# Cached attention of the sample streams with its operands swapped: queries stationary in four column groups

## The chip, the cores and the metric

The kernel runs on one core of a Trainium2 chip. The metric is the device time of one execution in microseconds. The kernel before was run three times: 2839.32, 2842.61 and 2842.74 us, median 2842.61 us.

## What is computed

One layer of a streaming encoder on two groups of tokens: a prompt of 256 tokens, and a sample group of 8 running streams with 16 new tokens each (128 rows together). All data is float32. The part that the change touches is the attention of the sample group over its cached keys and values:

```python
# sample group: 8 streams, 16 queries each, 128 cached keys and values per stream and head
kk = concatenate([cache_k, k])            # (8 streams, 128 + 16 keys, 8 heads, 128)
s  = einsum("bqhd,bkhd->bhqk", q, kk) / sqrt(128) + bias   # A: learned bias of the distance
s  = s + c_q - c_k                                         # B: sums of log forget gates
p  = softmax(s)                                            # over cached and own keys
y  = einsum("bhqk,bkhd->bqhd", p, concatenate([cache_v, v]))
```

There are 8 heads of kind A (bias by distance) and 8 of kind B (forget gates). After it come the gated branch projections, the output projection and, for every token, a mixture of experts: queries, keys, the best 16 of 256 candidates per retrieval head, and 128 gathered rows of two tables for each token.

## The kernel before

One core does everything, with an order written out by hand for each of the five engines and for the DMA queues, tied together by semaphores. `front(S)` (sample, 128 rows) comes first on TensorE, then `front(R)` (prompt, 256 rows); behind them stand the experts of the prompt. The sample's experts are worked on by VectorE between the steps of `front(R)`.

A front has four groups G of four heads each (G 0 and 1 are kind A, 2 and 3 kind B). A group needs three chunks of the input projection (queries, keys, values), each 2048 x 512 weights in four pieces of 1 MB that the sync queue loads into a ring of four (`wring`). A piece is four float32 matmuls with 512 moving columns (`part`, L600). The pieces of the next group's query and key chunks are laid between the attention steps of the present group by `fill()`, eight in all, so that TensorE has work while VectorE and ScalarE do the softmax.

For each head of the sample the steps are:

- `cached_scores(j)` (L661): for each of the 8 streams one matmul, with the stream's cached keys stationary (128 columns) and its 16 queries moving. The result lies with the keys on the partitions, in bank 3 of PSUM. For kind B, L659 first adds the sums of the cached forget gates.
- ScalarE copies that to `cst` (L994), and `scores(j)` turns it with an identity matmul into block 0 of bank 4 or 5 (L686), where L672 has put the scores of the new keys in block 1 and L683 the forget gates (kind B).
- `bias(j)` on VectorE adds biases and masks (L1327, or L1334 and L1335 for kind B) and takes the maximum of a row (L1343), ScalarE takes the exponent (L1000), `norm(j)` divides (L1352, L1355).
- `turn_probs(j)` (L698) transposes the two blocks of probabilities, ScalarE copies them (L1006), and `values(j)` (L716, L718) has the new values and then, for each stream, its cached values stationary with 16 probability columns moving. The result is already turned: ScalarE copies it to `yT` (L1012).

Two heads are in flight: the scores of head j+2 are made after the values of head j. Behind the last head of the front TensorE waits for `y_copied` and for the sigmoids of ScalarE (L1038) before it goes on to the branch projections.

GpSimd makes the masks at the start (`CONSTS` counts them) and loads the cached keys and values of the next group when `st_done` and `y_done` say that the present ones are used up (`load_caches`).

Of the kernel before, what the change touches and what calls it, by code (L numbers as in the profile page):

```python
# [52 lines left out]
CONSTS = 16  # L53
# [40 lines left out]
class Front:  # L94
# [3 lines left out]
    def __init__(self, sem, name, tiles, chunk0, streams):  # L98
        self.tiles, self.n, self.tokens, self.chunk0, self.streams = tiles, len(tiles), len(tiles) * P, chunk0, streams
        self.v_bank = 1 if streams else 0  # L100
        self.blocks = 2 if streams else 3

        self.segments = [(0, 2)] if streams else [(0, 1), (1, 2)]
# [16 lines left out]
        self.st_done = sem(f"st_done_{name}")  # L120
        self.st_copied = sem(f"st_copied_{name}")
# [7 lines left out]
        self.y_done = sem(f"y_done_{name}")  # L129
        self.y_copied = sem(f"y_copied_{name}")  # L130
# [68 lines left out]
def build(nc, a):  # L199

    with ExitStack() as ctx:
# [30 lines left out]
        cst = fold[:, 11 * P:13 * P].rearrange("p (w n) -> p w n", w=2)  # L232
# [13 lines left out]
        hnw = sb("hnw", [P, 2, HC])  # L246
        ranks = sb("ranks", [P, 2 * TOPK + 1], U32)
# [174 lines left out]
        def _(pool):  # L422
# [50 lines left out]
            def load_caches(G):  # L473
# [3 lines left out]
                for sm, dst, src, used in ((cache_loaded[0], ckT, a[k], S.st_done), (cache_loaded[1], cv, a[w], S.y_done)):  # L477
# [112 lines left out]
        def _(pe):  # L590
# [29 lines left out]
            def group(F, G, fill):  # L620
# [44 lines left out]
                def scores(j):  # L665
# [5 lines left out]
                    if F.streams:  # L671
                        mm(A[:, P:2 * P], q_of(j, 0), F.kT[:, j, :], start=True, stop=True, **sk)  # L672
                        f = F.lfb[:, 0, j, :] if br else None
                        extra = ((1, f, ntriB), (1, triB, f), (0, triB, f)) if br else ()
                    else:
                        mm(A[:, 0:P], q_of(j, 0), F.kT[:, j, 0:P], start=True, stop=True, **sk)
                        mm(A[:, P:3 * P], q_of(j, 1), F.kT[:, j, :], start=False, stop=True, **sk)
# [3 lines left out]
                    last = None  # L681
                    for m, left, right in extra:
                        last = mm(A[:, m * P:(m + 1) * P], left[:, :], right[:, :], start=False, stop=True, **sk)  # L683
                    if F.streams:
                        pe.wait_ge(F.st_copied, H + 1)
                        last = mm(A[:, 0:P], cst[:, j % 2, :], ident[:, :], start=False, stop=True, **sk)  # L686
                    elif last is None:

                        last = mm(A[:, 3 * P:3 * P + 1], ident[:, :], ident[:, 0:1], start=False, stop=True, **sk)
# [12 lines left out]
                def values(j):  # L702
                    H = H0 + j
                    pe.wait_ge(F.pt_copied, H + 1)
                    if H:
                        pe.wait_ge(F.y_copied, H)
# [19 lines left out]
                def score(j):  # L726
                    if F.streams:
                        cached_scores(j)
                    scores(j)

                score(0)
                if G == 1:
                    pe.wait_ge(F.z_ready, 1)
                score(1)
                fill()
                for j in range(HC):
                    turn_probs(j)
                    if j + 2 < HC:
                        if F.streams:
# [18 lines left out]
            def front(F):  # L758
# [13 lines left out]

                pe.wait_ge(F.y_copied, 2 * HEADS)
# [129 lines left out]
        def _(act):  # L903
# [35 lines left out]
            def front(F, experts):  # L939
# [14 lines left out]

                for G in range(2 * GROUPS):
                    H0, br, cols = HC * G, "ab"[G // GROUPS], slice((G % GROUPS) * CW, (G % GROUPS + 1) * CW)
                    for c in range(2):
# [7 lines left out]
                        if c:  # L965
                            place(2 * n * G, F.qT, F.turned, F.placed)
# [24 lines left out]
                    def copy_cached(j):  # L991
                        if F.streams:
                            act.wait_ge(F.st_done, H0 + j + 1)
                            act.activation(cst[:, j % 2, :], ps[:, 3, 0:P], ACT.Copy).then_inc(F.st_copied, 1)  # L994

# [755 lines left out]
```

## Time and profile before

| | |
|---|---|
| median of three runs | 2842.61 us (2839.32 to 2842.74) |
| span of the profiled execution | 2835.0 us |
| that execution's own time | not given apart from the three runs, which lie 4.3 to 7.7 us above the span |
| instructions | 19569 |
| TensorE busy | 2098.1 us (74%) |
| VectorE busy | 1870.1 us (66%) |
| GpSimd busy | 1254.9 us (44%) |
| ScalarE busy | 500.9 us (18%) |
| attention of the sample, by the rows of L661 and L718 | 66.7 to 314.2 us after the start |

PE is TensorE, PEld its weight loads, DVE is VectorE, ACT is ScalarE, POOL is GpSimd. A row of the timeline gives start and length in us, then engine, line, operation, output and inputs, and how many instructions were merged. A float32 matmul leaves two records of each kind, a transpose one. The ends of matmuls are modelled, so the step from one start to the next is the time that an instruction really takes from its followers. [...]

### The profile page before, as it was taken

Reading aid. Unit: us, or ns where it says so; the run is one execution under the profiler, and the core shown is the slowest. Engines: PE = TensorE matmul, PEld = TensorE weight load, DVE = VectorE, ACT = ScalarE, POOL = GpSimd, SP = SyncE. Lnnn points to the kernel's source line nnn. Section 1 sums busy time; section 2 is a strip of 40 time slices with the busy share of each in tenths; the row PEclk is TensorE's granted clock in tenths of the full one; section 3 lists DMA queues with packets and bytes.
Section 4 is the critical chain, followed back from the end, with each engine's and each line's share of the span. In section 5 each row is a group of like instructions: output and inputs, shape, how many; then the busy total and the mean of one; then the engine's idle time right before and its main releaser. Section 6 shows DMA issues by size and latency. Waiting matters only on the chain.

```text
span 2835.0 us, 19569 instructions
## 1 busy us (share of the span) xinstructions
PE 2098.1 (74%) x6070; PEld 1056.1 (37%) x6070; DVE 1870.1 (66%) x2615; ACT 500.9 (18%) x1187; POOL 1254.9 (44%) x855
## 2 busy tenths in 40 slices
PE   7999999999999898988899920000341038999996
PEld 3665544444545443333344410000331025444443
DVE  1222000396777757657666899999999998666666
ACT  1212100112222210000001100000995243000000
POOL 2000000023444445435444367776777866454444
PEclk9999999999999999989999965555555568999998
DMA  9777688989999999999999999999999998999999
GB/s 362 282 289 260 211 292 300 309 331 366 367 396 398 402 377 382 409 395 393 411 384 374 409 389 407 407 408 385 383 405 411 422 367 303 409 405 410 409 404 353
DMA packets 271465, 1047.11 MB, mean 369 GB/s; under 512 B 19856, under 2 KB 19856, under 8 KB 203280
## 3 DMA queue, kind: packets, MB, share of 16 engines
q0 software_dynamic: 113792, 697.85, 61.1%
q1 hardware_dynamic: 154880, 343.97, 33.3%
q10 hardware_dynamic: 2704, 4.21, 0.4%
q8 instruction: 44, 0.72, 0.1%
q14 instruction: 45, 0.37, 0.0%
HBM read 1036.50 MB, written 9.45 MB: 369 GB/s over the span
## 4 chain that ended last, share of the span: by engine, by line
PE 39%; DVE 25%; DMA 24%; POOL 5%; issue 5%; ACT 1%; POOLq 0%; SPq 0%; DVEq 0%; ACTq 0%
PE ps L600 34%; DMA yTr<-in_peer_v,fold 12%; DVE bigs L1612 7%; DVE bigr L1612 6%; DMA bigr<-in_w_br_a 4%; DVE hr L1643 3%; POOL bigr L571 3%; DMA bigr<-in_w_out 2%; DMA bigs<-in_peer_v,idxnow 2%; DVE spare L1612 2%; DMA bigr<-in_w_in 2%; DVE pwork L1425 1%; PE ps L661 1%; PE ps L718 1%; DVE bigs L1549 1%
## 5 line engine op out<-in xcount | busy, mean ns | idle before, releaser
L600 PE MATMUL ps<-bigr 128*128 128x512 f32 x1920 | 862.1, 607 | 43.5 <-DMA bigr<-in_w_in 21.7
L600 PEld LDWEIGHTS ps<-bigr 128*128 128x128 f32 x1920 | 368.3, 195 | 497.4 <-issue 442.7
L524 POOL DMA_INDIRECT bigs<-in_peer_u,idxnow x128 | 230.7, 1802 | 551.1 <-DVE bigs L1559 531.8
L600 PE MATMUL ps<-bigr,bigs 128*128 128x512 f32 x896 | 406.1, 608 | 20.3 <-DMA bigr<-in_w_in 16.7
L1643 DVE SCALAR_TENSOR_TENSOR hr<-yTr,fold,hr 128x1024 f32<-128x1024 f32 x205 | 263.5, 1286 | 136.8 <-DMA yTr<-in_peer_v,fold 134.4
L1549 DVE SCALAR_TENSOR_TENSOR bigs<-bigs,acts 128x2048 f32<-128x2048 f32 x128 | 300.9, 2350 | 67.4 <-DMA bigs<-in_peer_v,idxnow 67.1
L1559 DVE SCALAR_TENSOR_TENSOR bigs<-bigs 128x2048 f32<-128x2048 f32 x128 | 293.0, 2290 | 63.8 <-DMA bigs<-in_peer_u,idxnow 62.4
L581 POOL DMA_INDIRECT yTr<-in_peer_v,fold x205 | 219.6, 1071 | 207.0 <-DVE hr L1643 197.6
L1612 DVE SCALAR_TENSOR_TENSOR bigr<-bigr 128x2048 f32<-128x2048 f32 x122 | 275.8, 2288 | 5.9 <-DMA bigr<-in_peer_u,fold 5.2
L571 POOL DMA_INDIRECT bigr<-in_peer_u,fold x122 | 237.4, 1946 | 51.3 <-issue 35.5
L600 PEld LDWEIGHTS ps<-bigr,bigs 128*128 128x128 f32 x896 | 170.5, 195 | 218.5 <-issue 212.3
L524 POOL DMA_INDIRECT bigs<-in_peer_v,idxnow x128 | 211.9, 1655 | 50.8 <-issue 39.0
L1612 DVE SCALAR_TENSOR_TENSOR bigs<-bigs,bigr 128x2048 f32<-128x2048 f32 x96 | 214.9, 2287 | 0.6
L865 PE MATMUL ps<-ident,fold 128*128 128x128 f32 x2 | 1.0, 476 | 288.7 <-DVE fold L1618 288.7
L571 POOL DMA_INDIRECT bigs<-in_peer_u,fold x96 | 171.5, 1787 | 62.7 <-issue 25.3
L889 PE MATMUL ps<-spare,bigs 128*128 128x512 f32 x384 | 180.5, 592 | 0.7 <-ACT bigr L1186 0.7
L889 PE MATMUL ps<-spare,bigr 128*128 128x512 f32 x384 | 180.4, 592 | 0.0
L1380 DVE TENSOR_TENSOR bigr<-ps,bigr 128x512 f32<-128x512 f32 x24 | 15.8, 687 | 207.2 <-PE ps L600 207.2
L859 PE MATMUL ps<-ident,fold 128*128 128x128 f32 x4 | 1.4, 448 | 195.8 <-DVE fold L1517 195.8
L877 PE MATMUL ps<-normed,bigr 128*128 128x128 f32 x256 | 65.5, 437 | 101.5 <-issue 93.6
L600 PE MATMUL ps<-bigr,yTr 128*128 128x512 f32 x256 | 115.7, 613 | 14.5 <-DMA bigr<-in_w_br_a 11.2
L510 POOL IOTA fold<- 128x128 f32 x1 | 0.2, 242 | 257.3 <-DVE stage L1404 257.3
(261 smaller groups left out, 2228.8 us busy)
## 6 DMA issues: line engine op xcount, KB each, us to landing
bigr<-in_w_in SPq DMA_DIRECT2D x160, 1024.0 KB
spare<-in_peer_v SPq DMA_DIRECT2D x96, 512.0 KB
bigr<-in_w_out SPq DMA_DIRECT2D x32, 1024.0 KB
bigr<-in_w_pq SPq DMA_DIRECT2D x32, 1024.0 KB
bigr<-in_w_br_a SPq DMA_DIRECT2D x16, 1024.0 KB
bigr<-in_w_br_b SPq DMA_DIRECT2D x16, 1024.0 KB
bigr<-in_peer_v SPq DMA_DIRECT2D x32, 512.0 KB
bigr<-in_ckT_a POOLq DMA_DIRECT2D x2, 2048.0 KB, 9.9
```

The lines of the kernel that those rows point to most:

```text
L524: pool.indirect_dma_start(row, None, table[:, :], bass.IndirectOffsetOnAxis(ap=col, axis=0)).then_inc(loaded, 16)
L571: pool.indirect_dma_start(ER.urow[u], None, a["peer_u"][:, :], bass.IndirectOffsetOnAxis(ap=eidx[t][:, s:s + 1], axis=0)).then_inc(ER.u_lo ...
L581: pool.indirect_dma_start(ER.vrow[k % VBUF], None, halves, bass.IndirectOffsetOnAxis(ap=hidx[:, t, s:s + 1], axis=0)).then_inc(ER.v_loaded ...
L600: last = mm(ps[:, bank + t, :], src[:, k0 + k, t * P:(t + 1) * P], wring[:, s, k, :], start=(k0 + k == 0), stop=(k0 + k == kt - 1))
L661: last = mm(out[:, b * SQ:(b + 1) * SQ], ckT[:, j, b, :], q_of(j, 0)[:, b * SQ:(b + 1) * SQ], start=(not br and b == 0), stop=True, **sk)
L718: last = mm(Y[:, b * SQ:(b + 1) * SQ], cv[:, j, b, :], pt(0)[:, b * SQ:(b + 1) * SQ], start=False, stop=True, **sk)
L877: last = mm(ps[:, 4 + b, n * P:(n + 1) * P], hot_a[t][:, b, n, :], hot_i[:, b, n, :], start=(n == 0), stop=True, **sk)
L889: last = mm(ps[:, 2 * t + c, :], table[t][:, i, :], ER.dense[b][:, c * CW:(c + 1) * CW], start=(i == 0), stop=(i == P - 1))
L1549: dve.scalar_tensor_tensor(h, E.vrow[s], acts[:, s:s + 1], h, ALU.mult, ALU.add).then_inc(E.v_free, 1)
L1559: dve.scalar_tensor_tensor(E.urow[u], E.urow[u], 1.0, xn, ALU.mult, ALU.mult, accum_out=dots[:, s:s + 1]).then_inc(E.u_free, 1)
L1612: dve.scalar_tensor_tensor(ER.urow[u], ER.urow[u], 1.0, R.xn2[:, t, :], ALU.mult, ALU.mult, accum_out=rdots[:, t, s:s + 1]).then_inc(ER.u_ ...
L1643: dve.scalar_tensor_tensor(h, ER.vrow[v], gates[t][:, s:s + 1], h, ALU.mult, ALU.add).then_inc(ER.v_free, 1)
```

## The change

Queries and probabilities become the stationary operand and the cached keys and values the moving one. Stationary are the 32 columns that belong to two streams, so that four matmuls cover the 128 rows, each writing 32 partitions of PSUM. They stream the keys of both streams, so each row also gets scores against the keys of the other stream of its pair; a mask (`other`, made from `turns`) drops these. The scores have three blocks now (even stream, odd stream, new keys) in place of two, and one segment of 384 columns for the softmax. The scores need no copy and no turning; the result of the values comes out unturned and goes through `ys` and a transpose (`turn_y`, `place_y`).

```diff
-CONSTS = 16
+CONSTS = 19
-        self.blocks = 2 if streams else 3
-        self.segments = [(0, 2)] if streams else [(0, 1), (1, 2)]
+        self.blocks = 3
+        self.segments = [(0, 3)] if streams else [(0, 1), (1, 2)]
...
+            link(pool.memset(turns[:, :, :], 1.0))
+            link(select(turns[:, :, :], ALU.is_ge, 0, [[-SQ, 2], [-2 * SQ, STREAMS // 2]], 1, 0.0))
+            link(select(turns[:, :, :], ALU.is_gt, SQ, [[SQ, 2], [2 * SQ, STREAMS // 2]], -1, 0.0))
...
-                for sm, dst, src, used in ((cache_loaded[0], ckT, a[k], S.st_done), ...
+                for sm, dst, src, used in ((cache_loaded[0], ckT, a[k], S.s_done), ...
...
                 if G:
+                    if F.streams:
+                        turn_y(F, H0 - 1)
                     pe.wait_ge(F.pt_copied, H0)
-                    pe.wait_ge(F.y_copied, H0)
+                    pe.wait_ge(F.y_read if F.streams else F.y_copied, H0)
...
-                def cached_scores(j):
-                    if H0 + j:
-                        pe.wait_ge(F.st_copied, H0 + j)
-                    out = ps[:, 3, 0:P]
-                    if br:
-                        mm(out, stri[:, :], clfb[:, j, :, :].rearrange("p b n -> p (b n)"), start=True, stop=True)
-                    for b in range(STREAMS):
-                        last = mm(out[:, b * SQ:(b + 1) * SQ], ckT[:, j, b, :], q_of(j, 0)[:, b * SQ:(b + 1) * SQ],
-                                  start=(not br and b == 0), stop=True, **sk)
-                    last.then_inc(F.st_done, 1)
...
                     if F.streams:
-                        mm(A[:, P:2 * P], q_of(j, 0), F.kT[:, j, :], start=True, stop=True, **sk)
-                        f = F.lfb[:, 0, j, :] if br else None
-                        extra = ((1, f, ntriB), (1, triB, f), (0, triB, f)) if br else ()
+                        mm(A[:, 2 * P:3 * P], q_of(j, 0), F.kT[:, j, :], start=True, stop=True, **sk)
+                        if br:
+                            f = F.lfb[:, 0, j, :]
+                            mm(A[:, 2 * P:3 * P], f, ntriB[:, :], start=False, stop=True, **sk)
+                            mm(A[:, 0:3 * P].rearrange("p (m n) -> p m n", m=3), triB[:, :],
+                               f.unsqueeze(1).to_broadcast([P, 3, P]), start=False, stop=True, **sk)
+                            mm(A[:, 0:2 * P].rearrange("p (m n) -> p m n", m=2),
+                               clfb[:, j, :, :].rearrange("p b n -> p (b n)"),
+                               stri[:, :].unsqueeze(1).to_broadcast([P, 2, P]), start=False, stop=True, **sk)
+                        for g in range(STREAMS // 2):
+                            own = slice(2 * SQ * g, 2 * SQ * (g + 1))
+                            last = mm(ps[own, 4 + j % 2, 0:2 * P], q_of(j, 0)[:, own],
+                                      ckT[:, j, 2 * g:2 * g + 2, :].rearrange("p b n -> p (b n)"),
+                                      start=False, stop=True, **sk)
...
-                    if F.streams:
-                        pe.wait_ge(F.st_copied, H + 1)
-                        last = mm(A[:, 0:P], cst[:, j % 2, :], ident[:, :], start=False, stop=True, **sk)
...
                     if F.streams:
                         pe.wait_ge(cache_loaded[1], 16 * (G + 1))
-                        mm(Y[:, 0:P], vh(0), pt(1), start=True, stop=True, **sk)
-                        for b in range(STREAMS):
-                            last = mm(Y[:, b * SQ:(b + 1) * SQ], cv[:, j, b, :], pt(0)[:, b * SQ:(b + 1) * SQ],
-                                      start=False, stop=True, **sk)
+                        mm(Y[:, 0:P], pt(2), vh(0), start=True, stop=True, **sk)
+                        for m in range(2):
+                            for g in range(STREAMS // 2):
+                                own = slice(2 * SQ * g, 2 * SQ * (g + 1))
+                                last = mm(ps[own, 7, 0:P], pt(m)[:, own], cv[:, j, 2 * g + m, :],
+                                          start=False, stop=True, **sk)
...
                 for j in range(HC):
                     turn_probs(j)
-                    if j + 2 < HC:
-                        if F.streams:
-                            cached_scores(j + 2)
+                    if F.streams and j:
+                        turn_y(F, H0 + j - 1)
                     fill()
                     values(j)
...
+            def turn_y(F, H):
+                pe.wait_ge(F.y_read, H + 1)
+                if H:
+                    pe.wait_ge(F.y_copied, H)
+                pe.transpose(ps[:, 3, 0:P], ys[:, H % 2, :], ident[:, :]).then_inc(F.y_turned, 1)
...
+                if F.streams:
+                    turn_y(F, 2 * HEADS - 1)
                 pe.wait_ge(F.y_copied, 2 * HEADS)
...
+                def place_y(H):
+                    act.wait_ge(F.y_turned, H + 1)
+                    act.activation(F.yT[:, H // HEADS, H % HEADS, :], ps[:, 3, 0:P], ACT.Copy).then_inc(F.y_copied, 1)
...
-                            act.activation(cst[:, j % 2, :], ps[:, 3, 0:P], ACT.Copy).then_inc(F.st_copied, 1)
...
                         act.wait_ge(F.y_done, H + 1)
+                        if F.streams:
+                            if H >= 2:
+                                act.wait_ge(F.y_turned, H - 1)
+                            act.activation(ys[:, H % 2, :], ps[:, 7, 0:P], ACT.Copy).then_inc(F.y_read, 1)
...
+                    dve.wait_ge(made, CONSTS)
+                    link(dve.tensor_reduce(other[:, :], turns[:, :, :], AX, ALU.add))
+                    link(dve.tensor_scalar(other[:, :], other[:, :], -1.0, -MASKED, ALU.add, ALU.mult))
...
                         if F.streams and not br:
-                            dve.tensor_tensor(two(X), two(A[:, 0:2 * P]), biasS[:, :, h, :], ALU.add
-                                              ).then_inc(F.biased, 1)
+                            for s in range(2):
+                                step(dve.scalar_tensor_tensor(X[:, s * P:(s + 1) * P], A[:, s * P:(s + 1) * P],
+                                                              other[:, s:s + 1], biasS[:, 0, h, :], ALU.add, ALU.add))
+                            dve.tensor_tensor(X[:, 2 * P:3 * P], A[:, 2 * P:3 * P], biasS[:, 1, h, :], ALU.add
+                                              ).then_inc(F.biased, 1)
...
                         elif F.streams:
-                            step(dve.tensor_copy(X[:, 0:P], A[:, 0:P]))
-                            dve.tensor_tensor(X[:, P:2 * P], A[:, P:2 * P], maskO[:, :], ALU.add).then_inc(F.biased, 1)
+                            step(dve.tensor_tensor(two(X[:, 0:2 * P]), two(A[:, 0:2 * P]),
+                                                   other[:, :].unsqueeze(2).to_broadcast([P, 2, P]), ALU.add))
+                            dve.tensor_tensor(X[:, 2 * P:3 * P], A[:, 2 * P:3 * P], maskO[:, :], ALU.add
+                                              ).then_inc(F.biased, 1)
```

## Rows read from the trace of the kernel before

**Rows 1.** The page: span, and busy time of TensorE and the others

```profile
span 2835.0 us, 19569 instructions
PE 2098.1 (74%) x6070; PEld 1056.1 (37%) x6070; DVE 1870.1 (66%) x2615; ACT 500.9 (18%) x1187; POOL 1254.9 (44%) x855
```

**Rows 2.** Windows: us, busy time of each engine, granted clock, DMA share, GB/s

```profile
66.00:97.00 31.00, 30.95 (x158) 21.41 (x157) 5.39 (x17) 5.51 (x15) 0.54 (x1) 0.94 0.68 250
...
134.00:165.00 31.00, 30.95 (x157) 21.01 (x156) 5.64 (x19) 6.03 (x17) 0.54 (x1) 0.94 0.64 224
...
198.00:230.00 32.00, 32.00 (x188) 23.49 (x187) 5.80 (x22) 5.67 (x16) 0.54 (x1) 1.00 0.72 266
...
313.00:540.00 227.00, 217.70 (x535) 97.76 (x535) 17.14 (x27) 15.90 (x23) 1.94 (x4) 0.99 0.86 289
```

**Rows 3.** Groups by line and form, 64 to 316 us, TensorE and its weight loads

```profile
L600 PE MATMUL ps<-bigr,bigs 128*128 128x512 f32 x351 | 163.1, 611 | 1.7 <-DMA bigr<-in_w_in 1.0 <-ACT bigs L976 0.7
L661 PE MATMUL ps<-bigs,bigr 128*128 128x16 f32 x256 | 29.9, 258 | 0.0
L718 PE MATMUL ps<-pwork,yTr 128*128 128x16 f32 x256 | 29.7, 258 | 0.0
...
L661 PEld LDWEIGHTS ps<-bigs,bigr 128*128 128x128 f32 x256 | 30.2, 193 | 1.0 <-issue 1.0
```

**Rows 4.** Timeline of TensorE, one head of kind A (G 0, j = 0 and 2)

```profile
76.68 0.38 PE L698 MATMUL ps<-ident,pwork 128*128 128x128 f32 x2
76.90 1.86 PE L661 MATMUL ps<-bigs,bigr 128*128 128x16 f32 x16
78.61 3.68 PE L600 MATMUL ps<-bigr,bigs 128*128 128x512 f32 x8
82.12 0.38 PE L716 MATMUL ps<-pwork,bigs 128*128 128x128 f32 x2
82.34 1.86 PE L718 MATMUL ps<-pwork,yTr 128*128 128x16 f32 x16
84.05 0.47 PE L672 MATMUL ps<-bigs 128*128 128x128 f32 x2
84.35 0.39 PE L686 MATMUL ps<-ident,fold 128*128 128x128 f32 x2
84.58 3.60 PE L600 MATMUL ps<-bigr,bigs 128*128 128x512 f32 x8
```

**Rows 5.** Timeline of TensorE, what kind B has beside that (G 2)

```profile
219.91 0.39 PE L659 MATMUL ps<-fold 128*128 128x128 f32 x2
...
227.58 0.39 PE L683 MATMUL ps<-fold,bigs 128*128 128x128 f32 x2
227.81 0.61 PE L683 MATMUL ps<-bigs,fold 128*128 128x128 f32 x4
228.25 0.39 PE L686 MATMUL ps<-ident,fold 128*128 128x128 f32 x2
```

**Rows 6.** Timeline of TensorE, first head of G 0, the wait for the copy

```profile
68.44 0.47 PE L672 MATMUL ps<-bigs 128*128 128x128 f32 x2
68.96 0.49 PE L686 MATMUL ps<-ident,fold 128*128 128x128 f32 x2
```

**Rows 7.** Windows, behind the scores of the second head of G 0

```profile
72.00:75.00 3.00, 3.00 (x7) 1.49 (x8) 2.03 (x7) 2.18 (x5) 0.00 (x0) 0.64 0.11 38
```

**Rows 8.** Timeline of VectorE, second head of G 2, start and end of the softmax

```profile
204.28 0.29 DVE L1334 COPY pwork<-ps 128x128 f32<-128x128 f32 x1 [2.05 <-PE ps L686]
...
205.65 0.35 DVE L1355 TENSOR_SCALAR pwork<-pwork,rinv 128x256 f32<-128x256 f32 x1
```

**Rows 9.** Timeline of ScalarE and TensorE, end of the sample's attention

```profile
314.23 0.28 ACT L1012 ACTIVATE bigs<-ps 128x128 f32<-128x128 f32 x1 [4.97 <-PE ps L718]
...
316.76 5.68 PE L600 MATMUL ps<-bigr,bigs 128*128 128x512 f32 x9 [2.57 <-ACT bigr L1038]
```

**Rows 10.** Timeline of GpSimd, first work after the masks

```profile
27.82 0.61 POOL L470 DMA_DIRECT2D bigr<-in_relC  x1 [15.90 <-PE ps L600]
```

More of the change, by code:

```diff
@@ L119, in __init__ @@
         self.lfb_ready = sem(f"lfb_ready_{name}")
-        self.st_done = sem(f"st_done_{name}")
-        self.st_copied = sem(f"st_copied_{name}")
         self.s_done = sem(f"s_done_{name}")
@@ L129, in __init__ @@
         self.y_done = sem(f"y_done_{name}")
+        self.y_read = sem(f"y_read_{name}")
+        self.y_turned = sem(f"y_turned_{name}")
         self.y_copied = sem(f"y_copied_{name}")
@@ L246, in build @@
         hnw = sb("hnw", [P, 2, HC])
+        turns = sb("turns", [P, 2, STREAMS // 2])
+        other = sb("other", [P, 2])
         ranks = sb("ranks", [P, 2 * TOPK + 1], U32)
@@ L476, in load_caches @@
                 k, w = (("ckT_a", "cv_a"), ("ckT_b", "cv_b"))[G // GROUPS]
-                for sm, dst, src, used in ((cache_loaded[0], ckT, a[k], S.st_done), (cache_loaded[1], cv, a[w], S.y_done)):
+                for sm, dst, src, used in ((cache_loaded[0], ckT, a[k], S.s_done), (cache_loaded[1], cv, a[w], S.y_done)):
                     if G:
@@ L671, in scores @@
                     if F.streams:
-                        mm(A[:, P:2 * P], q_of(j, 0), F.kT[:, j, :], start=True, stop=True, **sk)
-                        f = F.lfb[:, 0, j, :] if br else None
-                        extra = ((1, f, ntriB), (1, triB, f), (0, triB, f)) if br else ()
+                        mm(A[:, 2 * P:3 * P], q_of(j, 0), F.kT[:, j, :], start=True, stop=True, **sk)
[12 more added lines that the diff above has]
+                                      start=False, stop=True, **sk)
                     else:
                         mm(A[:, 0:P], q_of(j, 0), F.kT[:, j, 0:P], start=True, stop=True, **sk)
-                        mm(A[:, P:3 * P], q_of(j, 1), F.kT[:, j, :], start=False, stop=True, **sk)
+                        last = mm(A[:, P:3 * P], q_of(j, 1), F.kT[:, j, :], start=False, stop=True, **sk)
                         f0, f1 = (F.lfb[:, t, j, :] for t in range(2)) if br else (None, None)
@@ L680, in scores @@
                                  (2, tri, f1)) if br else ()
-                    last = None
-                    for m, left, right in extra:
-                        last = mm(A[:, m * P:(m + 1) * P], left[:, :], right[:, :], start=False, stop=True, **sk)
-                    if F.streams:
-                        pe.wait_ge(F.st_copied, H + 1)
-                        last = mm(A[:, 0:P], cst[:, j % 2, :], ident[:, :], start=False, stop=True, **sk)
-                    elif last is None:
-                        last = mm(A[:, 3 * P:3 * P + 1], ident[:, :], ident[:, 0:1], start=False, stop=True, **sk)
+                        for m, left, right in extra:
+                            last = mm(A[:, m * P:(m + 1) * P], left[:, :], right[:, :], start=False, stop=True, **sk)
+                        if not br:
+                            last = mm(A[:, 3 * P:3 * P + 1], ident[:, :], ident[:, 0:1], start=False, stop=True, **sk)
                     last.then_inc(F.s_done, 1)
@@ L705, in values @@
                     if H:
-                        pe.wait_ge(F.y_copied, H)
+                        pe.wait_ge(F.y_read if F.streams else F.y_copied, H)
                     Y = ps[:, 7, :]
@@ L724, in values @@
                     last.then_inc(F.y_done, 1)
-                def score(j):
-                    if F.streams:
-                        cached_scores(j)
-                    scores(j)
-                score(0)
+                scores(0)
                 if G == 1:
                     pe.wait_ge(F.z_ready, 1)
-                score(1)
+                scores(1)
                 fill()
@@ L965, in front @@
                         if c:
+                            if G and F.streams:
+                                place_y(H0 - 1)
                             place(2 * n * G, F.qT, F.turned, F.placed)
@@ L1011, in copy_y @@
                         act.wait_ge(F.y_done, H + 1)
[L1012 to L1013 removed]
+                        if F.streams:
+                            if H >= 2:
+                                act.wait_ge(F.y_turned, H - 1)
+                            act.activation(ys[:, H % 2, :], ps[:, 7, 0:P], ACT.Copy).then_inc(F.y_read, 1)
+                        else:
+                            act.activation(F.yT[:, H // HEADS, H % HEADS, :], ps[:, 7, 0:F.tokens], ACT.Copy
+                                           ).then_inc(F.y_copied, 1)
                     if G == 1:
@@ L1023, in front @@
                         copy_probs(j)
-                        if j + 2 < HC:
-                            copy_cached(j + 2)
+                        if F.streams and j:
+                            place_y(H0 + j - 1)
                         copy_y(j)
@@ L1031, in front @@
                         prepare(R)
+                if F.streams:
+                    place_y(2 * HEADS - 1)
                 for i in range(NCH):
```

10 lines of the change are left out of this document (1 added, 9 removed).

## The prediction

> **What bounds the kernel now.** The page comes first. Its totals name no single bound: TensorE is busy for 74% of the span, VectorE for 66% [rows 1]. The change touches only the sample's attention, so the windows of that stretch come next. There TensorE is busy for 30.95 of 31 us and 32.00 of 32, while VectorE and ScalarE have 5 to 6 us each and the transfers a share of 0.64 to 0.72 [rows 2]. TensorE bounds the stretch, and time taken from it there is time gained. The groups by line show what it does: 256 records of L661 and 256 of L718 beside the projection's L600 [rows 3]. Behind the stretch TensorE goes on with 217.7 us of 227 [rows 2], and the experts' work needs its results, so nothing absorbs a shift. I take it over one to one.
>
> **What a record costs.** From the timeline, start to start: 16 records of L661, eight matmuls with 16 columns moving, take 76.90 to 78.61 = 1.71 us, 0.107 a record, and L718 the same [rows 4]. The two 128-column transposes of L698 take 0.22, also 0.11 each, and a matmul of 128 moving columns (L716) 0.22 for its two records. Four matmuls of 512 columns take 78.61 to 82.12 = 3.5 us, 0.43 a record [rows 4]. So time follows the moving columns from 128 upward (0.107 us per 128 and record), and a narrow one pays as much as 128, which is its stationary load of 128 columns. The kernel before streams 16 and pays for 128.
>
> **Part by part, if matmuls still run one after another.** Kind A, before: L698 0.22, L661 1.71, L716 0.22, L718 1.71, L672 0.30, L686 0.23, together 4.39 us [rows 4]. After: three transposes 0.33, one of `turn_y` 0.11, new keys 0.22, new values 0.22, four of 256 columns 8 x 0.215 = 1.72, eight of 128 columns 1.71, together 4.31. Kind B, before, adds L659 0.22 and the three L683 0.23 + 0.44 [rows 5], 5.26 in all; after, the gates are one of 128, one of 384 and one of 256 columns, 0.22 + 0.64 + 0.43, 5.60 in all. Eight heads each: 8 x (-0.08 + 0.34) = +2.1 us. So the swap by itself saves nothing: it streams 16 times as many columns in half as many matmuls for the scores, and eight times as many for the values.
>
> The waits. L686 starts 0.52 us after L672 in the first head against 0.30 in the third, where a projection piece hides the copy by ScalarE [rows 4, 6]; that wait of 0.22 goes, at two heads of each of G 0 and 1, some -0.9 us. New: `turn_y(2)` of a group comes right behind `values(2)` and three transposes. The copy round trip is those 0.52 us and the transposes hide 0.33, so 0.2 a group, +0.8. At the end TensorE waited 2.57 us for ScalarE's copy, table and sigmoid [rows 9]; now a second copy (0.28) and a transpose with two signals stand ahead, +0.7. Together +0.6.
>
> Costed at nothing: VectorE's longer softmax. From bias to scaled probabilities takes 1.7 us (204.28 to 206.00) [rows 8]; with 384 columns for 256 I estimate 2.3. What hides it is the projection piece of 3.5 us behind the scores; if it took over 3.4, `turn_probs` would wait. ScalarE's wider exponents and copies, and `place_y`, lie in the same pieces. GpSimd's three operations lie in its 15.9 idle us [rows 10]. Its load of cached keys now waits for `s_done`, a few us later; behind it in the queue is only the load of values, which waits for `y_done` anyway, and the keys are wanted one group later. The sync queue's pieces are released by the same L600 as before.
>
> **Two prices that no row has.** First, whether matmuls with 32 stationary columns in different columns of the array overlap. Every record of the trace is 128 by 128 and follows its predecessor at the full step, so the rows bound it only: nothing overlaps (3.43 us a head for both sets), or all four run at once (a quarter, 0.86). I take a value between. [...]
>
> [...]
>
> Second, what the array pays to change between full width and 32 columns: four changes a head, 64 in all. From below, a mere change of shape: L672 behind L661 costs 0.30 where its records need 0.21, so 0.09. [...] 64 x 0.20 = +12.8 us (5.8 to 23.7).
>
> [...]
>
> **The clock.** [...] Both G 0 and G 1 show 0.94 over 31 us, G 2 has 1.00 [rows 2]: 6% of 31 is about 1.8 us lost in each. Wider streams may keep the clock up; I take half, -1.7 (0 to -3.5).
>
> **The sum.** 2.1 + 0.6 - 22.4 + 12.8 - 1.7 = -8.6 us, taken as -9. The profiled execution spans 2835.0 us, and the runs lie 4.3 to 7.7 us above that; I count from the median, 2842.6, to 2833.6. This case's own range: with changes at 0.09 and the clock's full gift -17.4, with 0.37 and no gift +4.0, so 2825 to 2847. It breaks even at 0.33 us a change.
>
> **Rivals.**
> - *No overlap.* TensorE streams the 32-column matmuls of the scores and the values one after another, at the step of its other records, and the changes of width come on top: 2.1 + 0.6 + 12.8 = +15.5, less up to 1.7 of clock: 2857 (2849 at 0.09 a change, 2869 at 0.37). It speaks for it that no record in the trace ever started ahead of the full step. It decides as soon as overlap gives less than the changes cost, that is under 1 us a head.
> - *Full overlap.* All four column groups run at once, both records too: 0.86 a head, -2.57 x 16 = -41 in place of -22.4, so -27: 2815. [...]
> - *The softmax becomes the wait.* Scores that are ready sooner and a softmax of over 3.4 us would make `turn_probs` wait, 16 times by up to 0.5 us: +8 on the forecast, 2842. The margin of 1.1 us [rows 4, 8] speaks against.
>
> **How the numbers follow.** Partial overlap 0.47, no overlap 0.36, full overlap 0.14, softmax 0.03. The range takes in both other cases' centres: 2815 to 2858. A measurement of this kernel can tell about 0.2%, 5.7 us, from no change. Faster by more: seven tenths of the first case (changes under 0.25 us) and full overlap, 0.47. Slower by more: nearly all of no overlap, and the worst changes, 0.37. Within: 0.16. The range of the likeliest case alone stands above.
>
> **What would show it.** In the timeline of a kind A head, from the first start to the start of what follows: the scores' eight narrow records 1.1 us (1.7 without overlap, 0.4 with all), the values' sixteen 1.0 (1.7, 0.4). Records of L661 and L686 are gone, forms with 128*32 stand in their place. L600 behind a narrow set starts 0.2 us late. The stretch to the first L600 after the attention ends at 308 in place of 316.8. No wait of TensorE for VectorE appears in the heads. I am wrong if the narrow records step by their full time, if a change costs over 0.33 us, or if the saving shows at 308 us and is gone at the end.

## The result and the profile after

| | before | after |
|---|---|---|
| median of the runs, us | 2840.97 (4 runs) | 2810.82 (4 runs) |
| ratio, with 95% interval | 1 | 0.9893 (0.9878 to 0.9908) |
| span of the profiled execution, us | 2835.0 | 2808.3 |
| from the first scores of G 0 to the branch projections, us | 66.7 to 316.8, 250.0 | 67.3 to 288.2, 220.9 |

The changed kernel is 30 us faster, 1.07%. Run again in two later sets it stood at 0.9895 (0.9873 to 0.9916) and 0.9907 (0.9883 to 0.9931). The forecast was 9 us, and the range ended at 2815.

The saving lies where it was looked for. The spans of the two profiled executions differ by 26.7 us, and the attention of the sample is 29.1 us shorter. The 2.4 us between the two numbers lie within what one and the same kernel varies by behind the attention (last experiment). The timeline of TensorE in the changed kernel, behind the first scores of G 0 (start, length in us, then the operation; to compare with [rows 4]):

```profile
69.13 3.70 PE L605 MATMUL ps<-bigr,bigs 128*128 128x512 f32 x8
72.67 0.49 PE L699 MATMUL ps<-ident,pwork 128*128 128x128 f32 x3
72.99 3.60 PE L605 MATMUL ps<-bigr,bigs 128*128 128x512 f32 x8
76.43 0.38 PE L717 MATMUL ps<-bigs,pwork 128*128 128x128 f32 x2
76.74 0.64 PE L721 MATMUL ps<-yTr,pwork 128*32 128x128 f32 x16
77.32 0.49 PE L667 MATMUL ps<-bigs 128*128 128x128 f32 x2
77.74 0.64 PE L678 MATMUL ps<-bigr,bigs 128*32 128x256 f32 x8
78.31 3.70 PE L605 MATMUL ps<-bigr,bigs 128*128 128x512 f32 x8
```

The form 128*32 means that 32 stationary columns are in use. Eight records of 256 columns in this form (L678) take 0.57 us from their start to that of what follows, and sixteen of 128 columns (L721) take 0.58. The two sets of sixteen narrow records of [rows 4] took 1.71 each. A record of 512 columns takes 0.43, so one of 256 should take 0.215 (an estimate), and eight one after another 1.72. That they run side by side is tested below.

Kind B pays for its wider gates as costed: 0.22 for L670, 0.65 for the 384 columns of L671, 0.53 for L673 with the change of width behind it. The same view in G 2:

```profile
194.82 0.39 PE L670 MATMUL ps<-fold,bigs 128*128 128x128 f32 x2
195.04 0.81 PE L671 MATMUL ps<-bigs,fold 128*128 128x384 f32 x2
195.69 0.59 PE L673 MATMUL ps<-fold 128*128 128x256 f32 x2
196.22 0.64 PE L678 MATMUL ps<-bigr,bigs 128*32 128x256 f32 x8
```

The windows (us, busy time of PE, PEld, DVE, ACT and POOL, granted clock as a share of full speed, DMA share, GB/s) show two more things than [rows 2]:

```profile
66.00:97.00 31.00, 31.00 (x163) 15.17 (x162) 8.39 (x28) 5.99 (x18) 0.54 (x1) 1.00 0.85 299
122.00:153.00 31.00, 31.00 (x163) 15.17 (x162) 8.55 (x29) 8.56 (x21) 0.54 (x1) 1.00 0.89 324
175.00:182.00 7.00, 6.30 (x10) 2.76 (x11) 0.00 (x0) 0.00 (x0) 0.00 (x0) 0.57 1.05 399
```

The first two stretches hold the first scores of G 0 and G 1, and the granted clock stays at 1.00 in both, where it had fallen before (0.64 over 72 to 75 us [rows 7]). At the start of G 2, with the transfers at a share of 1.05, the granted clock is down to 0.57. There TensorE now waits for weights, and at the end for the copy of the last result:

```profile
175.70 6.30 PE L605 MATMUL ps<-bigr,bigs 128*128 128x512 f32 x8 [3.89 <-DMA bigr<-in_w_in]
...
285.26 0.33 PE L749 MATMUL ps<-ident,fold 128*128 128x128 f32 x1 [0.40 <-ACT fold L1023]
288.16 13.97 PE L605 MATMUL ps<-bigr,bigs 128*128 128x512 f32 x32 [2.57 <-ACT bigr L1052]
```

Eight records that need 3.5 us from their start to that of what follows took 6.1 here. The kernel before waited 0.97 us at this place:

```profile
194.27 3.67 PE L600 MATMUL ps<-bigr,bigs 128*128 128x512 f32 x8 [0.97 <-DMA bigr<-in_w_in]
```

### The profile page after: what moved, and what is told of

Same layout as the page of the kernel before. It is cut to its first block, busy times and chain, and to the rows that moved or that the text cites. A ratio compares the mean times of both kernels' runs of the same rounds, so it can differ in the third digit from the quotient of the medians.

```text
span 2808.3 us, 19332 instructions
## 1 busy us (share of the span) xinstructions
PE 2063.6 (73%) x5926; PEld 1007.9 (36%) x5926; DVE 1877.7 (67%) x2633; ACT 503.0 (18%) x1187; POOL 1253.6 (45%) x858
## 4 chain that ended last, share of the span: by engine, by line
PE 39%; DVE 26%; DMA 24%; issue 5%; POOL 5%; ACT 1%; SPq 0%; POOLq 0%; DVEq 0%; ACTq 0%
PE ps L605 35%; DMA yTr<-in_peer_v,fold 13%; DVE bigs L1634 7%; DVE bigr L1634 6%; DMA bigr<-in_w_br_a 4%; DVE hr L1665 3%; POOL bigr L576 3%; DMA bigr<-in_w_out 2%; DVE spare L1634 2%; DMA bigs<-in_peer_v,idxnow 2%; DMA bigr<-in_w_in 2%; DVE pwork L1447 1%; DVE bigs L1571 1%; DMA bigs<-in_peer_u,idxnow 1%; POOL spare L576 1%
## 5 line engine op out<-in xcount | busy, mean ns | idle before, releaser
L605 PE MATMUL ps<-bigr 128*128 128x512 f32 x1920 | 862.6, 608 | 46.3 <-DMA bigr<-in_w_in 19.1
L605 PEld LDWEIGHTS ps<-bigr 128*128 128x128 f32 x1920 | 368.8, 195 | 500.1 <-issue 449.2
L605 PE MATMUL ps<-bigr,bigs 128*128 128x512 f32 x896 | 401.0, 601 | 26.5 <-DMA bigr<-in_w_in 22.9
L605 PEld LDWEIGHTS ps<-bigr,bigs 128*128 128x128 f32 x896 | 168.2, 193 | 226.6 <-issue 218.3
L1402 DVE TENSOR_TENSOR bigr<-ps,bigr 128x512 f32<-128x512 f32 x24 | 15.8, 688 | 201.8 <-PE ps L605 201.8
L605 PE MATMUL ps<-bigr,yTr 128*128 128x512 f32 x256 | 116.5, 617 | 13.0 <-DMA bigr<-in_w_br_a 9.7
L576 POOL DMA_INDIRECT spare<-in_peer_u,fold x38 | 86.7, 2282 | 59.2 <-DVE spare L1634 53.1
```

What stands on the lines that cost most here:

```text
L576: pool.indirect_dma_start(ER.urow[u], None, a["peer_u"][:, :], bass.IndirectOffsetOnAxis(ap=eidx[t][:, s:s + 1], axis=0)).then_inc(ER.u_lo ...
L605: last = mm(ps[:, bank + t, :], src[:, k0 + k, t * P:(t + 1) * P], wring[:, s, k, :], start=(k0 + k == 0), stop=(k0 + k == kt - 1))
L1402: dve.tensor_tensor(F.gate[:, s, t, :], ps[:, 2 * s + t, :], F.gate[:, s, t, :], ALU.mult).then_inc(F.prod_ready, 1)
```

## The experiments

Theory A says that each column group has a stream of its own and that the four run side by side. Theory B says that a matmul with a narrow stationary operand is cheap by itself. Theory C keeps what the author assumed for the forecast's -22.4 us, staggered pairs: the first record of a group starts beside the second of the group ahead of it, 2.04 us a head, with something else hiding what they cost. They go with a strict order of issue, in which a record that waits for its columns holds up all behind it; the third run tests that order by itself. All lengths of sets below are from the start of the set to the start of what follows.

### One column group for all, and one group alone

The first run puts all tiles into one column group:

```diff
-last = mm(ps[own, 4 + j % 2, 0:2 * P], q_of(j, 0)[:, own],
+last = mm(ps[0:2 * SQ, 4 + j % 2, 0:2 * P], q_of(j, 0)[:, own],
...
-last = mm(ps[own, 7, 0:P], pt(m)[:, own], cv[:, j, 2 * g + m, :],
+last = mm(ps[0:2 * SQ, 7, 0:P], pt(m)[:, own], cv[:, j, 2 * g + m, :],
```

> All four matmuls of the scores, and all eight of the values, write PSUM partitions 0 to 31, that is they use one column group; number, shapes and moving columns are those of the changed kernel. Left out by this: the cached part of the attention of rows 32 to 127 (and four small matmuls stand once at the start, so that these rows hold numbers; under 1 us). Theory A (column groups run side by side, records of one group follow one another): the eight score records take 8 x 0.215 = 1.7 us in place of 0.57, the sixteen of the values 1.7 us in place of 0.57, and the kernel is 16 x 2.3 = 36 us slower than the changed one, about 2847. Theory B (a matmul with 32 stationary columns is simply four times as fast, one after another): both sets stay at 0.57 us and the kernel stays at 2811. Theory C (as forecast, staggered pairs, but something else hides it): no change of the sets either, 2811.

The second computes only the first of the four groups, in the scores and in the values:

```diff
-for g in range(STREAMS // 2):
+for g in range(1):
```

> Only the first column group of four is computed, for the scores and the values; left out is the cached part of the attention of rows 32 to 127 (the same four small matmuls at the start as in the run with one shared group). Theory A (side by side): two score records of 0.215 us are as long as eight in four groups, so a set stays at about 0.55 us, the values likewise, and the kernel stays within 2 us of 2811. Theory B (cheap one by one): a set falls by three quarters of 0.43 us, 0.25 us remain, 16 x 2 x 0.32 = 10 us less, about 2801.

Measured, one run each: 2841.1 us with one shared group, 2811.7 with one group alone, beside 2832.4 for a run of the kernel before. The timeline of TensorE with the shared group:

```profile
67.62 1.91 PE L683 MATMUL ps<-bigr,bigs 128*32 128x256 f32 x8
69.47 0.49 PE L672 MATMUL ps<-bigs 128*128 128x128 f32 x2
...
79.34 1.94 PE L726 MATMUL ps<-yTr,pwork 128*32 128x128 f32 x16
81.21 0.49 PE L672 MATMUL ps<-bigs 128*128 128x128 f32 x2
```

and with one group alone:

```profile
67.59 0.62 PE L683 MATMUL ps<-bigr,bigs 128*32 128x256 f32 x2
68.14 0.49 PE L672 MATMUL ps<-bigs 128*128 128x128 f32 x2
...
76.72 0.62 PE L726 MATMUL ps<-yTr,pwork 128*32 128x128 f32 x4
77.28 0.49 PE L672 MATMUL ps<-bigs 128*128 128x128 f32 x2
```

With the same instructions in one column group a set takes 1.85 us (scores) and 1.87 (values), and the attention is 257.7 us long, 36.8 more than in the changed kernel where 36 was expected. With three quarters of the instructions gone a set takes 0.55 and 0.56, as against 0.57 and 0.58 with all of them. Both are what theory A says, in numbers, and both rule out theory B. The three further groups cost 0.02 us together. Theory C is ruled out too: by it the sets would not have moved in the first run, and they did.

### Does the order of issue matter, and what does a set consist of

The values in the order of the groups:

```diff
-for m in range(2):
-    for g in range(STREAMS // 2):
+for g in range(STREAMS // 2):
+    for m in range(2):
```

> The eight matmuls of the values are issued group by group (both streams of a pair behind each other) in place of stream by stream. Nothing is left out. Theory A with a queue for each group that the records ahead of it don't hold up: the set stays at 0.57 us. A strict issue in order, where a record waits for its own group and holds up those behind it: four records of 0.107 in a row for each group, overlapping only at the seams, 13 steps of 0.107 = 1.4 us in place of 0.57, 13 us slower in all, 2824. Theory B: no change.

The eight matmuls of the values twice:

```diff
-for m in range(2):
+for m in (0, 1, 0, 1):
```

> The eight cached matmuls of the values are issued twice (the cached part of the attention then counts double). Theory A with full overlap: the second set adds 4 x 0.107 = 0.43 us a head with no further change of width, 0.57 becomes 1.00 us, +6.9 us in all, 2818; the rest of a set, 0.14 us, is then what leaving the mode costs within it. If most of the 0.57 were the price of changing the width, the second set would add much less than 0.43.

Measured: 2810.5 and 2811.4 us. The set of the values group by group, in the timeline:

```profile
78.40 0.66 PE L721 MATMUL ps<-yTr,pwork 128*32 128x128 f32 x16
78.99 0.49 PE L667 MATMUL ps<-bigs 128*128 128x128 f32 x2
```

and doubled:

```profile
76.29 1.08 PE L721 MATMUL ps<-yTr,pwork 128*32 128x128 f32 x32
77.30 0.49 PE L667 MATMUL ps<-bigs 128*128 128x128 f32 x2
```

0.59 us in the other order, 0.01 more than stream by stream: four records for one group do not hold up those for the next. So the strict order, by which the forecast priced the overlap, is ruled out. Doubling adds 1.01 - 0.58 = 0.43 us, four records of 0.107 at full overlap, and the attention grew from 220.9 to 228.3 us, 7.4 where 6.9 was expected. Over all the single run shows only 0.6 us of it; a single run cannot resolve that (see the last experiment). What is left of a set, 0.14 us, does not grow with its content: it is a part of the change of width. Where narrow records stand behind narrow ones it is not there: 16 records of the values take 0.44 us in the last version below, four steps of 0.107 being 0.43.

### Scores alone, and what the clock did

The values are those of the kernel before again, on three blocks of probabilities:

```diff
-mm(Y[:, 0:P], pt(2), vh(0), start=True, stop=True, **sk)
-for m in range(2):
-    for g in range(STREAMS // 2):
-        own = slice(2 * SQ * g, 2 * SQ * (g + 1))
-        last = mm(ps[own, 7, 0:P], pt(m)[:, own], cv[:, j, 2 * g + m, :], start=False, stop=True, **sk)
+mm(Y[:, 0:P], vh(0), pt(2), start=True, stop=True, **sk)
+for b in range(STREAMS):
+    last = mm(Y[:, b * SQ:(b + 1) * SQ], cv[:, j, b, :],
+              pt(b % 2)[:, b * SQ:(b + 1) * SQ], start=False, stop=True, **sk)
...
```

`turn_y`, `place_y` and the copy to `ys` are taken out, and ScalarE copies to `yT` as in the kernel before.

> Scores as in the changed kernel, values as before it (cached values stationary, 16 probability columns moving, the result already turned, no further transpose). By the steps of the changed trace a head of kind A takes 3.2 us in place of 4.4 before and 2.4 after, one of kind B 4.6 in place of 5.3 and 3.7: 8 x 1.2 + 8 x 0.63 = 14.6 us less than before, 13.6 more than after. Clock, theory D: the narrow score matmuls with 16 moving columns made the granted clock fall in G 0 and G 1; then no fall stands behind the first scores here either, and the attention is 18 us shorter than before. Rival E: narrow matmuls of any kind do it, the values' too; then falls remain in the attention and it is 15 us shorter or less.

> Scores alone swapped, now timed. In its one look the attention ended 19.2 us earlier than before and 7.8 to 9.4 us later than in the changed kernel, yet the whole took as long as the changed kernel, because the prompt's front was 7 to 13 us shorter. If that was disturbance (theory H), the timed kernel is 8 to 9 us slower than the changed one, 0.992 of the kernel before. If the prompt's front gives back what is saved ahead of it (theory I), the two stay equal, at 0.989.

The kernel before was profiled a second time:

> The kernel before, profiled a second time. Theory D (two sets of eight matmuls with 16 moving columns behind each other make the granted clock fall): falls of 3.4 us stand again behind the first scores of G 0 and G 1, near 71 and 139 us, or of at least one of them. If they were an accident of one profile, none is there. The stretch from the sample's first expert row to the end of the prompt's front took 1041 us in the first profile and 1032 to 1046 in nine profiles of kernels that do not differ in it; a second profile shows how far it moves with one and the same kernel: a few us if it is disturbance, under 1 us if it depends on the kernel alone.

Measured: scores alone took 2809.5 us in a single run and 2819.7 us (2812.9 to 2832.9) in a set of six, 0.9929 (0.9900 to 0.9957) of the kernel before. The changed kernel beside it took 2813.6 (2811.3 to 2821.3). Its interval, 0.9883 to 0.9931, overlaps that of scores alone, so the whole times do not show how the gain divides. The attention is 230.3 us long in the first profile of scores alone and 235.1 in the second, against 250.0 before and 220.9 in the changed kernel; the table in the last experiment says why the two differ, and gives some 16 us to the scores and 14 to the values.

The clock, in windows over the first scores of G 0 and G 1, for the second profile of the kernel before:

```profile
66.00:97.00 31.00, 30.90 (x157) 20.99 (x156) 5.16 (x17) 5.52 (x15) 0.54 (x1) 0.94 0.65 235
134.00:165.00 31.00, 30.95 (x148) 21.26 (x148) 5.40 (x18) 5.51 (x15) 0.54 (x1) 0.89 0.61 219
```

and for scores alone:

```profile
66.00:97.00 31.00, 31.00 (x141) 16.64 (x140) 8.39 (x28) 4.85 (x13) 0.54 (x1) 1.00 0.83 292
126.00:157.00 31.00, 31.00 (x138) 16.52 (x137) 8.56 (x29) 8.26 (x18) 0.54 (x1) 1.00 0.79 268
```

Both profiles of the kernel before have the lower clock in both stretches; here both stretches are at 1.00, although the values' matmuls of 16 moving columns (L718 before) are all there. What TensorE had done before it fell was two score sets behind each other, sixteen narrow matmuls, the first at 66.74 us and the last before 71.20; a set of values stands alone between pieces of projection, and no fall stands behind one. As to these two places, theory D fits. The swap gives back the two falls, of 3.4 us each at a granted clock of 0.50, 1.7 us each, and 1.7 more in the second profile, where the fall in G 1 lasts 6.8 us (136.3 to 143.1).

The rest is less simple. Behind the two first score sets of kind B the clock did not fall in the kernel before (1.00 in G 2 [rows 2]). And rival E is ruled out only as to the values: in some profiles the clock falls behind another narrow set, the 16 matmuls with 8 moving columns of the forget gates ahead of G 1 (L754 before, L758 in the changed kernel). A fall begins within 1 us of their end in one of the two profiles of the kernel before (121.96 us), in one of three of the changed kernel (112.12) and in one of two of scores alone (114.68), the one whose attention is 15 us shorter than before, as E had said. Why it falls there in one profile and not in the next stays open.

### The load that TensorE began to wait for

The 2 MB load of the prompt's input is issued at G 0 in place of G 2:

```diff
-if G == 2:
-    pool.dma_start(xTr[:, :, :], a["xTr"].rearrange("p (k n) -> p k n", k=KT)).then_inc(R.xT_loaded, 16)
...
 pool.dma_start(a[f"v_{br}"][2 * P:T, cols], S.v[:, 0, :]).then_inc(S.v_stored, 16)
+if G == 0:
+    pool.dma_start(xTr[:, :, :], a["xTr"].rearrange("p (k n) -> p k n", k=KT)).then_inc(R.xT_loaded, 16)
```

> The 2 MB load of the prompt's transposed input is issued by GpSimd behind the stores of G 0 in place of the start of G 2; nothing else. In the changed kernel TensorE waits 3.89 us for weights at the start of G 2 (0.97 in the kernel before) and then runs a piece at the lower clock, 6.3 us in place of 3.5. Theory F: that wait is this load beside the cached values and the stores, competing with weight pieces that TensorE now wants sooner; it goes, with the fall of the clock behind it, and the kernel is 4 to 6.6 us faster than the changed one. Rival G: the load only moves the wait to G 0 or G 1, or the time comes back later, where weights are waited for: within 2 us.

> The changed kernel once more, beside the others of this call, as their measure. 0.989 of the kernel before, some 30 us faster.

Measured: 2811.0 us (2802.6 to 2816.8) with the early load, 2808.7 (2804.2 to 2815.4) without. In the timeline the piece at the start of G 2:

```profile
174.26 3.70 PE L605 MATMUL ps<-bigr,bigs 128*128 128x512 f32 x8 [0.34 <-ACT bigs L989]
```

The wait of 3.9 us is gone and the piece takes its normal time: some 6 us less at this place. Theory F is right on the cause. Yet the attention is 218.1 us long in place of 220.9, only 2.8 less. The rest went to the clock in this one profile, in windows of the changed kernel (first) and of this one (second) behind the forget gates:

```profile
111.00:115.00 4.00, 4.00 (x18) 2.33 (x18) 2.36 (x8) 1.08 (x3) 0.00 (x0) 1.00 1.01 415
111.00:115.00 4.00, 4.00 (x16) 2.60 (x16) 1.73 (x4) 1.08 (x3) 0.00 (x0) 0.62 1.02 417
```

That fall costs 1.7 us. Another, at the start of G 3, lasts 6.8 us in place of 3.4. The changed kernel's third profile has both, without the early load, so they are no work of the load. The timed runs show nothing of the gain: the medians lie 2.3 us apart, within ranges of 14 and 11 us, so the runs do not decide between F and rival G on the whole.

### The early load and more work in column groups

The early load, and the new keys (kind A) and new values in column groups too, so that in kind A scores follow values without a change of width between them:

```diff
+if not br:
+    mm(ps[own, 4 + j % 2, 2 * P:3 * P], q_of(j, 0)[:, own], F.kT[:, j, :], start=True, stop=True, **sk)
...
-mm(Y[:, 0:P], pt(2), vh(0), start=True, stop=True, **sk)
-for m in range(2):
+for m in (2, 0, 1):
     for g in range(STREAMS // 2):
-        last = mm(ps[own, 7, 0:P], pt(m)[:, own], cv[:, j, 2 * g + m, :], start=False, stop=True, **sk)
+        last = mm(ps[own, 7, 0:P], pt(m)[:, own], vh(0) if m == 2 else cv[:, j, 2 * g + m, :],
+                  start=(m == 2), stop=True, **sk)
```

> The early load, and the new keys (kind A) and new values (both kinds) in column groups too, so that scores behind values need no change of width between them. By the measured steps a change into column groups costs 0.09, leaving a set 0.14 and the way back 0.10. In kind A the scores of heads 2 and 3 save 0.35 us each and the pair of the first heads 0.36: 1.06 a group, 2.1 us in two groups; kind B keeps its full-width gates and saves nothing. With the early load 6 to 9 us faster than the changed kernel. If a change of width were free and the 0.57 only the length of a set, the tiling of the new keys would give nothing and this kernel would equal the one with the early load alone.

> The changed kernel as the measure of this call: 0.989 of the kernel before.

> Early load and more work in column groups, timed again. Its attention ended 8.7 to 10.3 us earlier than that of the changed kernel, but it was only 2 us faster over all. Theory H: 6 to 9 us faster than the changed kernel, 0.986 of the kernel before. Theory I: within 2 us of the changed kernel, 0.989.

The values and the scores behind them, in the timeline from the second set of runs:

```profile
77.12 0.43 PE L723 MATMUL ps<-bigs,pwork 128*32 128x128 f32 x8
77.36 0.62 PE L723 MATMUL ps<-yTr,pwork 128*32 128x128 f32 x16
77.80 0.44 PE L679 MATMUL ps<-bigs 128*32 128x128 f32 x8
78.02 0.65 PE L681 MATMUL ps<-bigr,bigs 128*32 128x256 f32 x8
78.60 3.70 PE L605 MATMUL ps<-bigr,bigs 128*128 128x512 f32 x8
```

77.12 to 78.60 is 1.48 us, against 1.88 (76.43 to 78.31) in the changed kernel: the new values' eight records need 0.24 instead of 0.31, and between values and scores nothing is paid (77.36 to 77.80, 0.44 us for sixteen records, of which four steps of 0.107 are 0.43). Measured: 2806.5 us (2803.3 to 2808.5) beside 2808.7 in one set of runs, 2800.1 (2793.5 to 2813.6) beside 2813.6 in the other; 0.9878 (0.9858 to 0.9898) and 0.9859 (0.9830 to 0.9888) of the kernel before. Its median was below that of the changed kernel in both, by 2 us, which is not clear of noise, and by 13 us; the size over all stays open. Inside the attention the gain repeats: by the table below it is 1.9 and 2.0 us shorter than with the early load alone, where 2.1 was expected.

### How far a single profile can be trusted

Kernels whose prompt front is the same differ there. The sample's expert rows on VectorE (first start to last start) for scores alone, in its first and in its second profile:

```profile
L1562 DVE SCALAR_TENSOR_TENSOR bigs<-bigs x128: 2281/2291/2366, 559.4 to 1588.5; 128x2048 f32<-128x2048 f32 x128
```

```profile
L1562 DVE SCALAR_TENSOR_TENSOR bigs<-bigs x128: 2280/2291/2294, 562.4 to 1600.8; 128x2048 f32<-128x2048 f32 x128
```

One and the same kernel takes 1029.1 us and 1038.4 us for this stretch; the kernel before takes 1039.2 and 1042.0 in its two profiles. A single run that agrees with the changed kernel to a few us therefore proves nothing on the whole. Theory H (disturbance) fits scores alone, which in six runs was 6 us slower than the changed kernel, though not clear of noise. For the last version the first set of runs lies where theory I put it; the second, 13 us, lies beyond theory H's 6 to 9.

Inside the attention two things vary between profiles, and both can be read from the traces: the wait ahead of the first projection piece of G 2, and what TensorE loses at a granted clock of 0.50: half of the time at that clock in which it works, since the weight loads of L600 step by 0.86 us there (73.17 to 74.03 in the first profile of the kernel before) and by 0.43 at 1.00 (75.39 to 75.82). Taken out of the length, they leave nearly the same number for every profile of a kernel:

| | attention, us | wait at G 2 | lost at clock 0.50 | rest |
|---|---|---|---|---|
| before, two profiles | 250.0, 250.4 | 1.0, 1.1 | 6.7, 6.8 | 242.4, 242.5 |
| scores alone, two | 230.3, 235.1 | 1.7, 2.4 | 2.0, 6.1 | 226.7, 226.6 |
| changed kernel, three | 220.9, 220.8, 222.6 | 3.9, 3.6, 3.6 | 4.0, 4.2, 6.1 | 213.0, 213.0, 213.0 |
| early load | 218.1 | 0.3 | 4.8 | 213.0 |
| early load and more in column groups, two | 213.0, 217.0 | 0.3, 0.3 | 1.5, 5.7 | 211.1, 211.0 |

So the instructions themselves became 29.4 us shorter, 15.8 by the scores and 13.6 by the values. The wait and the clock change a single profile by up to 5 us more or less.

## Why the prediction was wrong

**What bounds the stretch: right.** TensorE had no wait in the heads, but for the copy in the first heads of a group before (0.2 us, which went as forecast), and the time taken from it came off the total nearly one to one (26.7 us of the span and 30 of the median for 29.1 of attention).

**The swap by itself saves nothing: right.** With no overlap the same instructions made the attention 257.7 us long, 7.7 more than before. The stationary load as the price of a narrow record is read from the weight loads of the kernel before: over the sixteen records that take 1.71 us from 76.90 on, they stand without a gap, where a load of L600 has 0.24 us of nothing ahead of it.

```profile
76.79 1.87 PEld L661 LDWEIGHTS ps<-bigs,bigr 128*128 128x128 f32 x16
```

The rival "no overlap" had its price, +15.5 less the clock, too high, for reasons given with the clock and the changes below. Two slips in this part change little: the rows of kind B add up to 5.28 and not 5.26, so that +2.1 should be +1.9; and the scores stream 16 times as many columns in each matmul, but 8 times as many in all.

**The overlap: the step that failed.** The sum takes -22.4 us for it, from 2.04 us a head. That was an assumption of the author, and no run shows it. Within a group records follow one another: one group alone needs 0.55 us for its two records with 256 columns, which is 0.14 of the change of width and 2 x 0.21, the full step of each. But groups do not wait for each other: all four take 0.02 us more than one, and the order of issue is worth 0.01. The overlap is full, 0.86 a head, 41 us in all, 18.7 more than forecast. That was the second rival, which I gave 0.14; its price, 2815, was 4 us off the measured median. Eight records took 0.57 us, against 1.85 in a shared group: 1.85 / 0.57 = 3.2 times as fast, or (1.85 - 0.14) / (0.57 - 0.14) = 4 without the change of width.

**The change of width: nearly right.** The sum's +12.8 us is 64 changes at 0.20, with 0.37 at the upper end of the range. Both were assumptions of the author, and no run shows either. The rows show 0.09 on the way in (L717 to L721 is 0.31 where its records need 0.22), 0.14 in the set and 0.10 on the way back (L605's eight records take 3.54 behind a set, 3.44 otherwise): 0.33 a pair, 0.17 a change, 10.6 us for 64. What TensorE does in that time no run shows. L600 paid 0.07 behind L661 before, too [rows 4] (3.51 us against that 3.44), so some of this is not new; I had left that out, about 1 us.

**The clock: right in kind, its size uncertain.** Both falls behind the first scores are gone, -3.4 us where half was taken. Over the whole attention the loss at the lower clock went from 6.7 us to 4.0, and to 6.1 in the changed kernel's third profile, by falls at other places.

**The waits.** The one behind the last head grew as costed: 0.40 for the transpose, and the sigmoid still 2.57 behind it. `turn_y` of the third head costs 0.47 for the transposes ahead of it instead of 0.32, the 0.2 expected. The softmax, costed at nothing, cost nothing. Not foreseen was the wait for weights in G 2, 2.9 us longer and with a piece at the lower clock behind it. The trace of the kernel before had the sign: 0.97 us of waiting there, with the transfers at full share in the window ahead:

```profile
180.00:185.00 5.00, 5.00 (x13) 2.13 (x13) 3.03 (x12) 1.67 (x3) 0.00 (x0) 1.00 1.07 446
```

The corrected sum: 1.9 + 0.6 - 41.1 + 10.6 - 1.0 for the part of the change that was there already, + 2.9 for the weights, and the clock's balance over the stretch (four falls before, one and a longer one behind the wait after), -2.7: -28.8 us, against 29.1 measured.

## What to carry to other kernels

In this kernel a matmul with 16 moving columns and 128 stationary ones took as long as one with 128 moving columns, 0.107 us a record. Where you find such a one, price the swap with the stationary operand cut into column groups: here four groups ran in the time of one, in float32 and in both orders tried, for about 0.33 us for going in and out, with eight records of 256 columns in 0.57 us instead of 1.85. Work that stands next to such a set can go into column groups as well: values and scores together took 1.48 us in place of 1.88. When TensorE is made faster, look for the next place where it waits for transfers at full share: here 2.9 us of the gain were paid back there. And before you compare single profiles, take out the waits and the falls of the clock that differ between profiles of one kernel.

## What was not expected of the hardware

- Four column groups together take 0.57 us for eight float32 records of 256 columns, one group alone 0.55 for its two.
- Records for a group that is busy do not hold up those for another: four in a row for each group, 0.59 us, against 0.58.
- The granted clock fell to 0.50 behind two sets of narrow matmuls in all four places where the two profiles of the kernel before have them in G 0 and G 1, and at none of these places with the swapped scores. Elsewhere it fell in some profiles of a kernel and not in others, worth 1.7 us a time.
